# Order of the three partial products of a weight tile in a split-precision projection

## The reference

```python
def conformer_mixer(h, w_in, conv_w, conv_b, ln_g, ln_b, w_out):
    proj = jnp.einsum('bsd,de->bse', h, w_in)
    a, b, z = jnp.split(proj, 3, axis=-1)
    u = a * jax.nn.sigmoid(b)
    ...
    return jnp.einsum('bse,ed->bsd', y, w_out)
def shared_kv(x, kv_norm, w_kv):
    ...
    kv = jnp.einsum('bsd,de->bse', rmsnorm(x, kv_norm), w_kv)
    parts = jnp.split(kv, 2 * N_GROUPS, axis=-1)
...
def dilated_mixer(h, w_in, w_out, kv, rel_bias):
    ...
    parts = jnp.split(jnp.einsum('bsd,de->bse', h, w_in), N_GROUPS + 1, axis=-1)
    ...
    return jnp.einsum('bse,ed->bsd', y, w_out)
```

## Time and profile before

| | before |
|---|---|
| median of 3 runs | 1475.08 us (1474.82 to 1475.2) |
| the profiled execution's own time | 1474.38 us |
| span of its trace | 1472.6 us |
| TensorE (PE) busy | 1442.6 us, 98% |
| weight loads (PEld) busy | 1401.1 us, 95% |
| VectorE (DVE) busy | 797.4 us, 54% |
| ScalarE (ACT) busy | 663.7 us, 45% |
| GpSimd (POOL) busy | 385.0 us, 26% |
| granted clock of TensorE | 0.997 |

### The profile page before, as it was taken

One profiled execution on the slowest core, in us unless ns is written; L12 is line 12 of the kernel. 1 busy time (PEld: TensorE's weight loads), 2 busy tenths in 40 slices (PEclk: granted clock), 3 DMA queues, 4 the chain that ended last, 5 costly groups with the idle time before them and its releaser, 6 DMA issues.

```text
span 1472.6 us, 26308 instructions
## 1 busy us (share of the span) xinstructions
PE 1442.6 (98%) x10611; PEld 1401.1 (95%) x10611; DVE 797.4 (54%) x1232; ACT 663.7 (45%) x909; POOL 385.0 (26%) x168
## 2 busy tenths in 40 slices
PE   6999999999999999999999999999999999999997
PEld 5999999988899999999999999999999999999786
DVE  3899998422445455454454544545545455454333
ACT  5444444675634344344443444434444344444443
POOL 5788888798300000000000000000000000000685
PEclk9999999999999999999999999999999999999999
DMA  9666666556696666666666656766567665673752
GB/s 269 174 193 178 179 193 179 168 199 201 171 272 181 169 182 184 179 177 164 182 191 177 181 156 182 198 176 182 149 180 199 181 182 146 178 199 96 263 195 86
DMA packets 455089, 268.50 MB, mean 182 GB/s; under 512 B 4491, under 2 KB 437211, under 8 KB 454668
## 3 DMA queue, kind: packets, MB, share of 16 engines
q1 hardware_dynamic: 454860, 267.96, 63.9%
q10 hardware_dynamic: 192, 0.05, 0.0%
HBM read 263.70 MB, written 4.29 MB: 182 GB/s over the span
## 4 chain that ended last, share of the span: by engine, by line
PE 87%; DVE 10%; DMA 1%; ACT 1%; issue 1%; ACTq 0%; SPq 0%; DVEq 0%
PE bank L403 17%; PE bank L404 17%; PE bank L405 17%; DVE bank L919 8%; PE bank L382 6%; PE bank L381 6%; PE bank L383 6%; PE bank L423 3%; PE bank L425 3%; PE bank L424 3%; PE bank L1335 1%; PE bank L1317 1%; PE bank L1327 1%; DMA raw<-b_w_out_dram 1%; PE bank L1338 1%
## 5 line engine op out<-in xcount | busy, mean ns | idle before, releaser
L346 POOL TENSOR_TENSOR w_lo<-raw,w_hi 128x1024 fp32r<-128x1024 f32 x160 | 384.1, 2412 | 1070.4 <-ACT w_hi L337 1056.4
L337 ACT ACTIVATE w_hi<-raw 128x1024 fp32r<-128x1024 f32 x382 | 398.6, 1059 | 527.9 <-PE bank L405 312.5
L403 PE MATMUL bank<-mem_a,w_hi 128*128 128x256 f32 x1536 | 433.1, 282 | 4.9 <-DVE mem_a L891 1.8
L346 DVE TENSOR_TENSOR w_lo<-raw,w_hi 128x1024 fp32r<-128x1024 f32 x224 | 270.1, 1224 | 306.6 <-ACT w_hi L337 306.5
L404 PE MATMUL bank<-mem_a,w_hi 128*128 128x256 f32 x1536 | 429.9, 280 | 0.0
L405 PE MATMUL bank<-mem_a,w_lo 128*128 128x256 f32 x1536 | 427.7, 278 | 0.0
L403 PEld LDWEIGHTS bank<-mem_a,w_hi 128*128 128x128 f32 x1536 | 288.5, 188 | 8.4 <-DVE mem_a L891 2.7
L404 PEld LDWEIGHTS bank<-mem_a,w_hi 128*128 128x128 f32 x1536 | 290.3, 189 | 0.1
L405 PEld LDWEIGHTS bank<-mem_a,w_lo 128*128 128x128 f32 x1536 | 288.5, 188 | 0.0
L403 PE MATMUL bank<-mem_b,w_hi 128*128 128x256 f32 x1024 | 287.7, 281 | 0.0
L404 PE MATMUL bank<-mem_b,w_hi 128*128 128x256 f32 x1024 | 286.0, 279 | 0.0
(11 more groups left out here) (156 smaller groups left out, 1286.4 us busy)
## 6 DMA issues: line engine op xcount, KB each, us to landing
raw<-w_kv_dram SPq DMA_DIRECT2D x96, 1024.0 KB, 6.0
raw<-b_w_in_dram SPq DMA_DIRECT2D x64, 1024.0 KB, 7.0
raw<-a_w_in_dram SPq DMA_DIRECT2D x47, 1024.0 KB, 5.8
raw<-a_w_out_dram SPq DMA_DIRECT2D x16, 1024.0 KB, 5.0
raw<-b_w_out_dram SPq DMA_DIRECT2D x16, 1024.0 KB, 5.1
bias<-bias_dram SPq DMA_DIRECT2D x16, 384.0 KB, 6.5
x_sb<-x_dram SPq DMA_DIRECT2D x4, 512.0 KB, 5.6
resid_dram<-x_sb SPq DMA_DIRECT2D x1, 2048.0 KB, 10.9
```

The lines of the kernel that those rows point to most:

```text
L337: nc.scalar.activation(w_hi[:, stream.half_slot(half), :], raw[:, slot, part:part + HALF], ACT.Copy).then_inc(hi_done, 1)
L346: eng.tensor_tensor(w_lo[:, stream.half_slot(half), :], raw[:, slot, part:part + HALF], w_hi[:, stream.half_slot(half), :].bitcast(F32), A ...
L403: nc.tensor.matmul(dst[:, 0:S], wide_hi, source(kt, 0), start=(kt == 0), stop=False)
```

## The change

The second and the third product of each tile change places. The sum of the three has the same terms. Before, the order was (hi weight, hi input), (hi weight, lo input), (lo weight, hi input). Now it is (hi weight, hi input), (lo weight, hi input), (hi weight, lo input). The wait ahead of the tile, the `start` flag on the first product, the `stop` flag on the third and the count of `mm_done` on the half's last product stay.

```diff
@@ -401,8 +401,8 @@
                     wide_hi = w_hi[:, slot, k * P:(k + 1) * P]
                     wide_lo = w_lo[:, slot, k * P:(k + 1) * P]
                     nc.tensor.matmul(dst[:, 0:S], wide_hi, source(kt, 0), start=(kt == 0), stop=False)
-                    nc.tensor.matmul(dst[:, 0:S], wide_hi, source(kt, 1), start=False, stop=False)
-                    mm = nc.tensor.matmul(dst[:, 0:S], wide_lo, source(kt, 0),
+                    nc.tensor.matmul(dst[:, 0:S], wide_lo, source(kt, 0), start=False, stop=False)
+                    mm = nc.tensor.matmul(dst[:, 0:S], wide_hi, source(kt, 1),
                                           start=False, stop=(kt == KT - 1))
                 return mm
```

## The result

The changed kernel takes 1482.49 us (median of 5 runs, 1481.37 to 1482.57) against 1475.08 us before; the ratio is 1.0048 with an interval of 1.0036 to 1.0059. It is slower by 7.4 us, clear of noise. The forecast of no change was wrong, and the time lies 0.5 us above the stated range.

What follows compares the result with a forecast made beforehand. TensorE bounds the kernel, busy 1442.6 of 1472.6 us. Four terms of 0 (work, waits, neighbouring weights, product beside load) left 1474.4 us, plus 0.7 to the median: 1475.1 us, range 1469.0 to 1482.0.

Steps and rivals of the forecast that it cites:

- The point from which the slower rival decides: Undisturbed slabs of queries and gate: starts 5.63 us or more apart, against 5.60 for no change.
- slower rival: Heads: new order settles into a costlier rhythm, 4.5 us; 1479.6 us, with layer 0 up to 1482.8; chance 0.28.
- "little": Layer 0: of a loss up to 2.3 us, only little would be covered by TensorE's 1.69 us left idle.
- Which product runs beside which load: Lines 403 to 405: new pairs of streamed input and loading weights cost 0, within 3 ns a tile either way.
- three readings: Lines 403 to 405: 1 ns steps belong to next load's kind, place in tile or input part; each sums to 837 ns.
- need not depend on the order: Undisturbed slabs in the heads: steady state is stable, its mean possibly the same for the same loads and inputs.
- bound of 3 ns a tile either way: Three matmuls of a tile: 834 to 840 ns around 837, from the shortest and longest line, 278 and 280 ns.
- bound of 5.4 us: Heads, 1792 tiles: 3 ns a tile gives at most 5.4 us more or less.
- slow bound: Whole kernel: at most 1482.8 us, with the layer 0 part of a loss included.
- the rhythm seen after the transposes: Slab after the nine transposes in a head: 5.64 us for 48 matmuls against 5.60, 0.04 us more.

Runs made afterwards that it cites:

- six orders: All orders of a tile's three products (before, changed, four more): slabs of 5.60 us with inputs hi, lo, hi; 5.67 with hi, hi, lo; 5.65 with lo, hi, hi.

## Why the prediction was wrong

**Right.** Half of the end is set by these three lines, no wait grew that would matter, the loads stayed 10611 and those of these lines at 188 ns, and repeated weights were no cheaper (six orders). The point from which the slower rival decides, 5.63 us a slab, was passed at 5.67. The loss counted fully in the heads, 4.7 us in 14 of them, and partly ahead of the second head: 2.05 us, some 0.34 of them in the first head. The other 1.7 us compare with 48 x 0.067 = 3.2 us for the slabs of layer 0 if nothing were hidden (an estimate from the undisturbed slabs), so about half was covered there, more than the "little" of the prediction.

**The step that failed** is the one under "Which product runs beside which load": "I take 0, which all three readings give." The three readings sorted matmuls by line, by kind of load and by input part, and took their means. The means of the lines, 280, 279 and 278 ns, hide what varies. In the mean over the undisturbed slabs of queries and gate, the starts of before lie from 112.5 to 120.8 ns apart, in a pattern of 12 matmuls that repeats with the four tiles after which the input parts are back at the same place within 256 bytes. None of the three lines has one price; each place in the pattern does. The swap kept the set of places and loads, changed the sequence in which the input parts stream, and so the pattern, whose mean went from 116.7 to 118.0 ns. The prediction looked for the cause in the pair of a product and the load beside it; the six orders show that the pairs count for nothing and the sequence of the inputs for all of it. That a mean over the same loads and inputs "need not depend on the order" was the wrong way to lean.

**The rule on the ports.** The prediction set beside the trace what the Trainium skill says ("SBUF — State Buffer", who interferes with whom), that the streamed operand and the weight loads have independent ports, by which the pair can't matter. As to the pairs, the six orders agree with it. But it gives no reason for what the places do: the same loads took 192 ns beside unshifted inputs and 188 beside shifted ones, and in the output projections where the streamed weights stayed and the loaded inputs moved, the distance went from 227 to 233 ns. Whether the two reads get in each other's way is not shown, since no run moved the weights.

**The sizes.** The bound of 3 ns a tile either way was short: a tile costs 3 x 1.4 = 4 ns more in undisturbed slabs. The slabs that follow the values, the transposes and the attention rose by only 0.03 to 0.04 us, since they were out of the good rhythm before too, so the heads came to 0.34 us each and stayed just within the bound of 5.4 us for 16. That this bound held is luck, for it was made of differences between mean record lengths, which say nothing of the cause. The slow bound, 1482.8 us, would have held the median; the range was cut at 1482.0. (The slower rival's own terms, 4.5 and 2.3 us, add up to 1481.9; 1482.8 needs the 5.4 us of the other bound.)

**The slower rival** had the right mechanism in part. It put it down to the rhythm seen after the transposes. The runs show two things: the steady rhythm itself depends on the sequence of places, and beside that one layout can settle in more than one rhythm. In the first slab of a head, which ran at 117.7 ns a matmul before already, the swap cost 0.03 us; in the undisturbed ones 0.07.

**What stays open.** The runs show that the order acts through where the input parts start: with all of them at one place it cost nothing, in three layouts, and with 16 unused columns its sign turned. They don't show how. Whether the start counts against the loaded weights, for itself, or against what other engines read and write at the time was not separated, nor what picks one of several rhythms, and so whether the swap changed the price of the sequence or only the rhythm in which it settles. Why 32 bytes is the cheap shift and 224 is not, and whether 256 bytes is the scale (the 128 byte shift differs from none, so it isn't 128 or less), isn't settled. No rule here predicts the mean of a new sequence.

## What to carry to other kernels

Where TensorE is full and each matmul has its own load, compare kernels by the distance of starts over a whole slab, not by mean lengths by line: some 1.4 ns a matmul in the undisturbed slabs was most of the effect. A reordering that keeps every instruction and every wait still changes the sequence of addresses that TensorE reads, so its price is to be measured, together with the layout it was tuned for. And look for several rhythms in one trace before counting on the best one.

## What the runs showed of the hardware

- Successive matmuls of 256 `float32r` columns, each with a load of a 128 by 128 tile, start 116.6 to 120.0 ns apart in the mean at the full clock, by where their operands start in memory: 5.76 us for 48 with all inputs unshifted, 5.60 with all inputs shifted by 32 bytes and the weights left in place.
- With 512 columns it is the other way: 227 ns where the loaded inputs are unshifted, 233 with 32 bytes.
- With all input parts at one place the distances can be perfectly even (120 ns each without shift) or vary (113 to 120 ns with 32 bytes).
- The same places gave 118.7 ns in one slab of a head and 116.6 ns in another, and 5.60 us a slab in one run and 5.65 in another that differed in what lies behind the inputs.
- Loading weights that are already there takes 188 to 189 ns, as the other loads of these lines, and saves no time of the following matmul: orders with and without such a pair take the same 5.60, 5.67 or 5.65 us a slab by the sequence of their inputs alone.
